# The tokens' RMS factors through DRAM instead of four transposes, and the last token block scaled and stored in quarters

## The reference, cut to what matters

```
h = rmsnorm(x, attn_norm_g);  proj = h @ w_in
y_conv = (u_b * short_conv(u_c * u_x, conv_w)) @ w_conv_out
y_attn = sliding_window_attention(q, k, v, sinks, rel_bias) @ w_attn_out
x  = x + (sigmoid(g_conv) * y_conv + sigmoid(g_attn) * y_attn) @ w_o
h2 = rmsnorm(x, mlp_norm_g)
x  = x + square(relu(h2 @ w_up)) @ w_down          # 1024 -> 4096 -> 1024
out = rmsnorm(x, final_norm_g)
rmsnorm(x, g) = x * rsqrt(mean(x * x) + 1e-6) * g
```

## Time and profile before

| | us |
|---|---|
| median of 3 runs (762.75 to 763.8) | 762.76 |
| the profiled execution, its own time | 763.45 |
| its span, first to last instruction | 761.7 |
| PE busy | 752.7 (99%) |
| DVE busy | 637.4 (84%) |
| ACT busy | 407.6 (54%) |
| POOL busy | 75.9 (10%) |

### The profile page before, as it was taken

One profiled execution on the slowest core, in us unless ns is written; L12 is line 12 of the kernel. 1 busy time (PEld: TensorE's weight loads), 2 busy tenths in 40 slices (PEclk: granted clock), 3 DMA queues, 4 the chain that ended last, 5 costly groups with the idle time before them and its releaser, 6 DMA issues.

```text
span 761.7 us, 11518 instructions
## 1 busy us (share of the span) xinstructions
PE 752.7 (99%) x4563; PEld 675.0 (89%) x4563; DVE 637.4 (84%) x752; ACT 407.6 (54%) x529; POOL 75.9 (10%) x113
## 2 busy tenths in 40 slices
PE   8999999999999999999999999999999999999996
PEld 7888888888888999999988899889998999899985
DVE  5766688889896979886869899998799869986997
ACT  7424554453644655636616786654555356445565
POOL 3201000101112001010010101010101000010102
PEclk9999999999999999999999999999999999999999
DMA  7727313131219876779736866777676767777702
GB/s 255 244 83 278 111 55 111 56 111 55 72 39 262 242 186 169 194 237 327 235 80 198 219 160 173 174 205 177 175 209 172 215 166 190 196 184 203 194 1 111
DMA packets 70451, 128.13 MB, mean 168 GB/s; under 512 B 2620, under 2 KB 26244, under 8 KB 70404
## 3 DMA queue, kind: packets, MB, share of 16 engines
q1 hardware_dynamic: 53040, 85.23, 33.8%
q0 software_dynamic: 17152, 41.96, 25.4%
q10 hardware_dynamic: 212, 0.28, 0.1%
HBM read 121.14 MB, written 6.32 MB: 167 GB/s over the span
## 4 chain that ended last, share of the span: by engine, by line
PE 97%; DVE 1%; DMA 1%; ACT 0%; issue 0%; SPq 0%; ACTq 0%; DVEq 0%
PE pair L848 37%; PE pair L875 24%; PE pair L651 10%; PE pair L653 10%; PE pair L652 10%; PE pair L698 2%; PE pair L673 1%; PE pair L672 1%; PE pair L682 1%; DMA xn<-in_x 1%; PE pair L744 1%; PE pair L746 0%; PE pair L745 0%; PE pair L800 0%; DVE home_lo L1698 0%
## 5 line engine op out<-in xcount | busy, mean ns | idle before, releaser
L1164 ACT ACTIVATE high<-home_raw 128x2048 fp32r<-128x2048 f32 x84 | 160.9, 1916 | 156.2 <-PE pair L848 88.7
L1698 DVE TENSOR_TENSOR home_lo<-home_raw,high 128x2048 fp32r<-128x2048 f32 x84 | 192.2, 2288 | 35.3 <-ACT high L1164 34.7
L651 PE MATMUL pair<-h,wgt 128*128 128x512 f32 x320 | 126.7, 396 | 0.0
L653 PE MATMUL pair<-h,wgt 128*128 128x512 f32 x320 | 124.9, 390 | 0.0
L652 PE MATMUL pair<-h,wgt 128*128 128x512 f32 x320 | 124.8, 390 | 0.0
L653 PEld LDWEIGHTS pair<-h,wgt 128*128 128x128 f32 x320 | 60.1, 188 | 13.0
L652 PEld LDWEIGHTS pair<-h,wgt 128*128 128x128 f32 x320 | 60.3, 188 | 11.5
L651 PEld LDWEIGHTS pair<-h,wgt 128*128 128x128 f32 x320 | 60.2, 188 | 11.5
L875 PE MATMUL pair<-high,s_hi_tile 128*128 128x512 f32 x280 | 70.1, 391 | 0.0
L875 PE MATMUL pair<-home_lo,s_hi_tile 128*128 128x512 f32 x280 | 69.7, 390 | 0.0
L875 PE MATMUL pair<-high,s_lo_tile 128*128 128x512 f32 x280 | 69.7, 389 | 0.0
(11 more groups left out here) (222 smaller groups left out, 1151.8 us busy)
## 6 DMA issues: line engine op xcount, KB each, us to landing
raw<-in_w_in SPq DMA_DIRECT2D x42, 512.0 KB, 4.8
home_raw<-in_w_up SPq DMA_DIRECT2D x16, 1024.0 KB, 5.5
home_raw<-in_w_down SPq DMA_DIRECT2D x16, 1024.0 KB, 5.1
home_raw<-in_w_up POOLq DMA_DIRECT2D x12, 1024.0 KB, 8.4
home_raw<-in_w_down POOLq DMA_DIRECT2D x12, 1024.0 KB, 8.5
home_raw<-in_w_conv_out SPq DMA_DIRECT2D x4, 1024.0 KB, 8.2
home_raw<-in_w_attn_out SPq DMA_DIRECT2D x4, 1024.0 KB, 5.2
home_raw<-in_w_in SPq DMA_DIRECT2D x4, 1024.0 KB, 5.4
```

Of the source, the lines that this page charges most:

```text
L651: mm(bank[j][:, :], wh, rhs[:, 0, k, :], start=(k == 0), stop=False)
L653: last = mm(bank[j][:, :], wl, rhs[:, 0, k, :], start=False, stop=(k == KT - 1))
L1164: a(high[n % 2][:, :], home_raw[home_of(s, name)][:, :], ACT.Copy).then_inc(m_hi, 1)
L1698: v.tensor_tensor(home_lo[home][:, :], home_raw[home][:, :], f32(high[n % 2][:, :]), ALU.subtract).then_inc(m_lo, 1)
```

## The change

The factors are no longer spread, transposed and copied. The 512 of them are stored to a DRAM tensor `factors_row` by a DMA of ACT, one element of 4 bytes at a time, and a second DMA of ACT reads them back as one row for all 128 partitions. `token_sums` and the root move ahead of one `low_part` and one `high_part`, and the reciprocal ahead of one `h2_low`. In the last token block each half becomes two quarters of 256 columns: DVE scales two, ACT two; SP stores three, ACT one.

```diff
-        rbc = place("rbc", [P, TB, P], offset=ty_at + 4 * T)
+        factors_row = nc.dram_tensor("factors_row", (TB, P), F32)
 # sync
-            for b, late in ((0, 1), (0, 0), (1, 1), (1, 0), (2, 1), (2, 0), (3, 1)):
+            def store_quarter(eng, c):
+                eng.dma_start(out[3 * P:TB * P, 256 * c:256 * c + 256],
+                              res[:, 3, 256 * c:256 * c + 256]).then_inc(out_done, 16)
+            for b, late in ((0, 1), (0, 0), (1, 1), (1, 0), (2, 1), (2, 0)):
...
-            sp.wait_ge(out_done, 16 * 2 * TB)
+            sp.wait_ge(out_late, 4)
+            store_quarter(sp, 0)
+            sp.wait_ge(out_early[3], 1)
+            store_quarter(sp, 2)
+            sp.wait_ge(out_late, 5)
+            store_quarter(sp, 1)
+            sp.wait_ge(out_done, 16 * (2 * TB + 2))
 # tensor
-            def row_transposes():
-                pe.wait_ge(rbc_ready, 1)
-                pe.wait_ge(h2_raw, 12)
-                for b in range(TB):
-                    last = nc.tensor.transpose(bank[7][:, b * P:(b + 1) * P], rbc[:, b, :], ident[:, :])
-                last.then_inc(rrow_t, 1)
-                    up_product(s, M5, True, between=(0, row_transposes) if s == 4 else None)
+                    up_product(s, M5, True)
-                if s == 5:
-                    pe.wait_ge(rrow_ready, 1)
 # scalar
                     h2_high(M5)
+                    act.wait_ge(rr2_step, 1)
+                    a(rr2[:, 0, :], ss2[:, 2, :], ACT.Sqrt, bias=eps[:, :], scale=1.0 / D).then_inc(rr2_step, 1)
                 high_part(s, M5)
                 if first:
-                    act.wait_ge(rr2_step, 1)
-                    a(rr2[:, 0, :], ss2[:, 2, :], ACT.Sqrt, bias=eps[:, :], scale=1.0 / D).then_inc(rr2_step, 1)
-                if first:
+                    act.wait_ge(rr2_step, 3)
+                    with nc.allow_non_contiguous_dma("a factor a token"):
+                        act.dma_start(factors_row.rearrange("b p -> p b"), rr2[:, 1, :]).then_inc(row_out, 16)
                     h2_high(M7)
                 else:
                     square(s, 0)
                 high_part(s, M7)
+                if first:
+                    act.wait_ge(row_out, 16)
+                    act.dma_start(rrow[:, :], bass.AP(factors_row[:, :].tensor, 0, [[0, P], [1, T]])).then_inc(rrow_in, 16)
                 copy_out(s, zc12, M6, -1.0)
                 if first:
-                    act.wait_ge(rrow_t, 1)
-                    a(rrow[:, :], bank[7], ACT.Copy).then_inc(rrow_ready, 1)
                     h2_high(M3)
...
-            scale_early(3)
-            act.wait_ge(out_early[3], 1)
-            act.dma_start(out[3 * P:TB * P, 512:D], res[:, 3, 512:D]).then_inc(out_done, 16)
+            act.wait_ge(gained_late, 2)
+            act.wait_ge(fin_step, TB)
+            for c in (512, 768):
+                a(res[:, 3, c:c + 256], res[:, 3, c:c + 256], ACT.Copy, scale=rms3[:, 2, 3:4]).then_inc(out_early[3], 1)
+            act.wait_ge(out_early[3], 2)
+            act.dma_start(out[3 * P:TB * P, 768:D], res[:, 3, 768:D]).then_inc(out_done, 16)
 # vector
                 v.reciprocal(rr2[:, 1, :], rr2[:, 0, :]).then_inc(rr2_step, 1)
-                dve.wait_ge(rr2_step, 3)
-                v.tensor_copy(rbc[:, :, :], rr2[:, 1, :].rearrange("p (b n) -> p b n", n=1).to_broadcast([P, TB, P])
-                              ).then_inc(rbc_ready, 1)
...
             h2_low(M6)
+            token_sums()
             low_part(4, M6)
-            token_sums()
+            token_factors()
             h2_low(M5)
-            token_factors()
             low_part(4, M5)
             sum_c11(4)
             h2_low(M7)
             low_part(4, M7)
-            dve.wait_ge(rrow_ready, 1)
+            dve.wait_ge(rrow_in, 16)
             relu(4, 0)
...
-            scale_late(3)
+            dve.wait_ge(fin_step, TB)
+            for c in (0, 256):
+                q = res[:, 3, c:c + 256]
+                v.scalar_tensor_tensor(out=q, in0=q, scalar=rms3[:, 2, 3:4], in1=gfin[:, c:c + 256],
+                                       op0=ALU.mult, op1=ALU.mult).then_inc(out_late, 1)
```

More of the change, by code:

```diff
@@ L338, in build @@
         h2_sums, h2_split, h2_ready = sem("h2_sums"), sem("h2_split"), sem("h2_ready")
-        ss2_ready, rr2_step, rbc_ready = sem("ss2_ready"), sem("rr2_step"), sem("rbc_ready")
-        rrow_t, rrow_ready = sem("rrow_t"), sem("rrow_ready")
+        ss2_ready, rr2_step = sem("ss2_ready"), sem("rr2_step")
+        row_out, rrow_in = sem("row_out"), sem("rrow_in")
         b11_in, b22_in = sem("b11_in"), sem("b22_in")
```

## The result

The changed kernel takes 776.32 us (median of 5, 774.49 to 777.08) against 763.15 before: ratio 1.0171, 95% interval 1.0159 to 1.0182. It is 13 us slower. The profiled execution took 774.49 us with a span of 772.8, 11.1 us more than the 761.7 of before. It is the fastest of the five: what the others lose beyond it is in no trace of this kernel.

The account below looks back on a forecast made before the run. The prediction took PE, busy 99% of the span, as the bound. Transposes -0.42 us and the end +0.1 us gave -0.3 us, so 762.4 us from the median of 762.76, range 761.7 to 763.8.

Parts of the forecast that it names:

- the landing of the store: Stage 4, ACT's store of the factors: 3.5 us from issue at 455.4, landing at 458.9, between 458.2 and 460.6.
- The load's landing: Stage 4, row load to 128 partitions: 2.8 to 4.2 us from 458.9, landing before DVE wants it at 463.16.
- the one who is late: Stage 4, DVE's relu(4, 0) waits for the row: reachable at 463.16, may start at 463.96 at latest; priced at 0.
- slow single-element store: Rival, 6%: the factors' store takes 6.2 to 7.6 us; at 7.6, +3.2 us, 765.7 us in all.
- slow broadcast: Rival, 5%: the row's load takes 6.9 us like gfin's, landing at 465.8: +1.84 us, 764.3 us in all.
- every microsecond beyond: Stage 4: each microsecond that relu starts after 463.96 costs PE a microsecond.
- The transposes: Stage 4, four transposes removed from PE: -0.42 us in full, as long as PE waits for nothing else.
- The end: Last block in quarters: set by bytes, half in 1 KB packets, +0.1 us (+0.06 by the skill's formula).
- The moves of sums, root and reciprocal: Stage 4, DVE and ACT: low part delayed at most 0.1 us, high part some 0.2 us, covered.
- ACT's queue issues a DMA while the ACTIVATE ahead of it runs: Stage 4, row load behind M7's high part: issued at 458.9 during the ACTIVATE, not at 460.75 after it.

Follow-up runs that it names:

- quiet_probe: Kernel before plus three extra ACT transfers in its quiet last stage: 4-byte-neighbour store 10.3 us, 16-byte-piece store 1.4, broadcast row load 3.2; executed once.
- row_16b: Changed kernel with the old end, each partition's factors stored as 16 contiguous bytes, so tokens get wrong factors: 763.27 us, ratio 1.0005.
- store_128: Changed kernel with the old end, only 128 single 4-byte elements stored and waited for, row then loaded from final_norm_g: 773.69 us, ratio 1.0143.
- load_only: Changed kernel with the old end and no store, the row loaded from final_norm_g at the same place: 763.34 us, ratio 1.0006.
- load_distinct: As load_only, but each partition reads its own 2 KB of x instead of all the same row: 762.93 us, ratio 0.9999.
- store_unwaited: As load_only, with the store of 512 single elements put back but no work waiting for it: 768.75 us, ratio 1.0080.
- load_early: As load_only, but the load is issued some 12 us earlier, while the DMA engines are idle: 762.71 us, ratio 0.9994.
- row_only: Changed kernel with the factors' round trip alone, without the quarters of the last block: 774.79 us, ratio 1.0150.

## Why the prediction was wrong

**The step that failed** is the landing of the store, "I take 3.5 us, between them and nearer the second": 10.0 us were measured, nearly twice its upper end of 5.2. I bounded a store of neighbouring 4-byte elements by a load with 4-byte elements (`rbt`) and by a store with 2 KB pieces (ACT's). Neither has the property that costs, small writes close together in DRAM (quiet_probe: 10.3 us against 1.4 for the same bytes in 16-byte pieces). With 2.8 us there, the kernel was level with before (row_16b). Near the 3.5 us lies the store of 512 elements 512 bytes apart, 2.9; what the sum lacked was a term for writes that neighbour each other.

**The load's landing**, "2.8 to 4.2 us", was 8.5 us, for two reasons. Some 5 us passed between its issue and its first packet, and this goes with the dense store ahead of it: store_128 has it too (over 3 us to the first packet, 7.9 in all, another row), load_only does not. Why, no run shows. Without that store it was 4.8 us (load_only), and there what was missing is that all partitions read one row: with 128 different places the load took 3.2 us (load_distinct), within the range. A row that hinted at it was cited, `gfin`'s 6.9 us, and set aside for the 1 MB ahead of it; what made that one slow no run shows.

**What was priced at nothing.** The effect on others: POOL's load took 16.0 us, or 15.1 without any wait for the store (store_unwaited, 5.7 us lost). And the text named only `relu` as the one who is late; but ACT's own stream stood at the store too, and its `copy_out` of `zc12` held PE 2.6 us before M7.

**Rivals.** The slow single-element store had 6% and the slow broadcast 5%, each by itself. The first came true and went beyond its 7.6 us and its 765.7; the second came true in part (4.8 us in load_only, where the rival had 6.9). That "every microsecond beyond" 463.96 "is a microsecond of PE" held: `relu` started at 473.59, which on the clock of the kernel before (whose stage 4 starts 0.35 us later) is 473.94, 9.98 us late, and PE stood 9.92 in all. What came on top, 1.5 us, was the clock, which has no term in the prediction: it fell during the stand before M3, and PE's first group after it took 3.41 us in place of 1.92. The Trainium skill's sentence on transfers below 512 B (page "DMA: Bandwidth & Descriptors", section "Specifications") speaks of reading, modifying and writing, and I could not price it. The traces agree that small stores can be slow, yet 512 elements 512 bytes apart took 2.9 us and 16-byte pieces 1.4, so size alone does not decide.

**The transposes**, -0.42 us: right, 79.70 to 79.28 and 79.29 us in load_distinct and load_early. In load_only they were taken back by POOL's late load.

**The end**: right in direction, with the engines full to the last packet as forecast, but mis-sized: +0.3 us; both sizes that the prediction worked out, 0.1 and 0.06, are too small. Of it 0.17 us fit the lower rate of the 1 KB packets. The moves of sums, root and reciprocal cost PE nothing, as forecast; the store was issued at 455.02 (forecast 455.4, which is 455.05 with the same 0.35 us taken off). That ACT's queue issues a DMA while the ACTIVATE ahead of it runs was right too, as load_only's timeline shows:

```profile
458.48 1.92 ACT L1154 ACTIVATE high<-home_raw 128x2048 fp32r<-128x2048 f32 x1 [2.08 <-PE pair L840]
458.49 0.37 ACTq L1357 DMA_DIRECT2D rrow<-in_final_norm_g  x1
```

## What to carry to other kernels

Turning a column of partitions into a row through DRAM by single 4-byte elements puts the densest possible small writes into a short stretch of DRAM, which took 10 us here: store each partition's values as one piece (16 bytes were enough here: 1.4 in place of 10.3 us), or space them, and reorder on the way back. A row broadcast to all partitions is one DRAM row read 128 times; if another load starts beside it, a few copies of the row can be worth trying (3.0 in place of 4.8 us). Here the repaired round trip still gained nothing that the time shows. Bound an operation by rows that share its access pattern, not only its bytes, its count or its queue; and when a wait is put into an engine's stream, price everything behind it on that engine.

## What the runs showed of the hardware that I had not expected

- The landing of a store of 512 single 4-byte elements with idle DMA engines: 4 bytes apart 10.3 us, 8 apart 4.7, 16 apart 2.8; 128 neighbours 9.8 (8.0 beside other loads); 16-byte pieces 1.4. The time passes after the packets: in the changed kernel the store's last packet was at 457.4, and the semaphore came at 465.0.
- Beside such a store POOL's accumulating load crawls, at 14 to 123 GB/s, until 2.6 us after the store's landing, and takes 15 to 16 us in place of 8.3. Loads of ACT and SP issued within a microsecond of the landing had their first packets 5 to 6 us after their issue.
- 128 reads of one 2 KB row as an accumulating load starts (load_only): 61 to 97 GB/s in sum; 128 different places did not do it, nor did four copies of the row (load 3.0 us, POOL's 8.5).
- TensorE's clock fell during a stand of PE (changed kernel) or just after one (row_only), and the work after it paid: after stands of 7.1 us (changed kernel) and 2.3 and 5.7 us (row_only) the next group took 0.7 to 1.7 us more than its 1.92. After the 2.5 us before M7 in the changed kernel it took 0.10 more, at a clock of 1.00.
